# A chunked recurrence's scores: 128-key products against products of 32 keys, scores cleared once

## The chip, the cores and the metric

One core of one Trainium2 chip. The metric is the time of one execution on the device in microseconds (us), the median of the runs; lower is better.

## What is computed

One layer of a trunk on x (1, 2048, 1024), in f32: a normalised input projection into differential attention and a gated linear recurrence, an output projection, and a gated feed-forward layer. The recurrence is the part that the change touches:

```python
# per head, chunks of tokens; b = cumulative log of the forget gate, k = 1 - f
diff   = b[t] - b[s]
decay  = exp(where(t >= s, diff, -inf))
scores = einsum('tk,sk,tsk->ts', q, k, decay)
o      = einsum('ts,sv->tv', scores, v) + einsum('tk,kv->tv', q * exp(b), state)
state  = exp(b_last) * state + einsum('sk,sv->kv', k * exp(b_last - b), v)
```

There are 4 heads of 128 features. The kernel takes chunks of 128 tokens, 4 heads wide.

## The kernel before

The kernel has four stages in a row: `project` (input projection), `mix_tokens` (attention and recurrence, the stage of the change), `feed` (output projection and feed-forward) and `down`. Each stage has one program for each engine, written out by hand, and counted semaphores between them; an engine does its list in order. SyncE (SP) issues the DMAs.

**Attention in `mix_tokens`.** `for s in range(TOTAL + 2)` runs over 4 heads x 16 steps of 128 queries. In a step TensorE makes the scores of two maps (`score`, L1396 to L1399: f32r products with up to 512 keys into a ring of four PSUM banks; L1398 adds the chunk mask by a product of 64 loaded columns), VectorE takes maxima (L1259), ScalarE exponentials (L1148), VectorE combines the two maps (L1278), TensorE turns them (L1413), ScalarE copies them (L1157), and TensorE weighs the values (L1424).

**Recurrence in the same stage.** While attention works on head h (16 steps), the recurrence works on block h of 512 tokens (4 chunks of 128, all 4 heads). Its work is cut into 30 "fills", each of which TensorE writes into one PSUM bank and another engine reads. `FILLS` (L780) lists them: 4 diagonals, 7 levels x 2 sides (a side is 2 heads, so 8 head-chunks), 4 turned keys, and 4 pairs of output and state. Two fills go into each of the first 15 steps (`fill(h, 2 * j)` between the two maps' scores, `fill(h, 2 * j + 1)` after the first turns). For the first 8 fills of a block two banks are used in turn, `rec_fill` and the spare bank of the ring (in the trace `att_ring`); later ones have one bank.

The scores of a chunk are made by levels. At level m, j = 2^m: the queries in the right half of each run of 2j tokens meet the keys in the left half of the same run. GpSimd multiplies keys and queries in place by the forget factors between levels (L1127, L1129), and waits for the fill before (`fill_done`). TensorE (`fill`, L1441) makes for each of the 8 head-chunks one product: all 128 keys are loaded, and the 64 queries of the right halves are moved. Only at the last level (m = 6, L1464) are just 64 keys loaded. VectorE (`read_fill`, L1281) then writes the valid part into `rscore` by a predicated copy with a mask of the level (L1298); at the last level it is a plain copy (L1296). The diagonal fill (L1453) is 128 keys by 128 queries for each of a head's 4 chunks, and VectorE multiplies it by the identity (L1288), which writes the whole tile and so also clears it.

The lines that set the reading:

```python
tok = slice(c * C, (c + 1) * C)
queries = rq[:, head, tok].rearrange("p (n s j) -> p n s j", s=2, j=1 << at)[:, :, 1, :]
if at == LEVELS - 1:
    earlier = slice(c * C, c * C + RUN)
    last = pe.matmul(out[0:RUN, hc * RUN:(hc + 1) * RUN], rk[:, head, earlier], queries, start=True, stop=True)
    continue
dst = out[:, hc * RUN:(hc + 1) * RUN].rearrange("p (n j) -> p n j", j=1 << at)
last = pe.matmul(dst, rk[:, head, tok], queries, start=True, stop=True)
```

TensorE may write a fill when `fill_read` says that the one (or the one before) has been read. An f32 product appears in the trace as two pairs of a weight load (PEld) and a matmul (PE). In a product `matmul(out, lhsT, rhs)` lhsT is what is loaded, rhs what is moved. The trace writes "128\*64" for 128 rows and 64 loaded columns.

**Start of the stage.** VectorE clears `state` (L1340), makes `early_rows` and `late_keys` (L1341 to L1345, the small operands of L1398), then the two products for lambda (L1348). TensorE's first instruction waits for `masks_made` = 4, which the last of these memsets brings.

**Masks.** `make_level_masks` (L128), on GpSimd at the start of `project`, makes 7 masks of 128 x 512 bytes. GpSimd's next work in `project` waits for pieces of `w_out` (L492).

## Time and profile before

| what | value |
|---|---|
| median of 3 runs | 2718.12 us (2717.34 to 2718.37) |
| the profiled execution | 2718.51 us |
| its span | 2716.8 us |
| instructions | 34334 |
| mean granted TensorE clock | 0.987 |

All times below are from the one profiled execution. PE is TensorE's matmuls, PEld its weight loads (which overlap them), DVE is VectorE, ACT ScalarE, POOL GpSimd. A timeline row merges neighbouring instructions of one kind; its second number reaches from the first one's start to the last one's end, and x16 says how many. Matmuls are pipelined and their ends are modelled, so the distance between starts tells more than the duration of one. The clock is given as a share of full speed (2.4 GHz), and 0.50 is 1.2 GHz.

### The profile page before, as it was taken

Reading aid. Unit: us, or ns where it says so; the run is one execution under the profiler, and the core shown is the slowest. Engines: PE = TensorE matmul, PEld = TensorE weight load, DVE = VectorE, ACT = ScalarE, POOL = GpSimd, SP = SyncE. Lnnn points to the kernel's source line nnn. Section 1 sums busy time; section 2 is a strip of 40 time slices with the busy share of each in tenths; the row PEclk is TensorE's granted clock in tenths of the full one; section 3 lists DMA queues with packets and bytes.
Section 4 is the critical chain, followed back from the end, with each engine's and each line's share of the span. In section 5 each row is a group of like instructions: output and inputs, shape, how many; then the busy total and the mean of one; then the engine's idle time right before and its main releaser. Section 6 shows DMA issues by size and latency. Waiting matters only on the chain. (4 is left out here: it accounts for less than half of the span.)

```text
span 2716.8 us, 34334 instructions
## 1 busy us (share of the span) xinstructions
PE 2609.6 (96%) x13288; PEld 2202.3 (81%) x13288; DVE 1555.9 (57%) x1915; ACT 1141.3 (42%) x1917; POOL 906.2 (33%) x607
## 2 busy tenths in 40 slices
PE   7999999999899999997998999999999999999999
PEld 6888888887888888885877888887888887888887
DVE  5434344333676767675566666667666666356653
ACT  4434344332577676775554222224222223332221
POOL 5001100001515151403546445554554452236400
PEclk9999999999999999997999999999999999999999
DMA  4755556384443433306685333345343335777763
GB/s 159 263 184 194 177 201 202 124 273 126 121 111 94 123 96 101 109 21 216 228 278 169 95 103 108 101 116 183 101 116 96 103 109 158 262 271 275 238 204 130
DMA packets 343874, 430.48 MB, mean 158 GB/s; under 512 B 19232, under 2 KB 212768, under 8 KB 341024
## 3 DMA queue, kind: packets, MB, share of 16 engines
q1 hardware_dynamic: 343712, 428.29, 49.9%
q8 instruction: 106, 1.74, 0.3%
q14 instruction: 56, 0.46, 0.1%
HBM read 301.87 MB, written 129.50 MB: 159 GB/s over the span
## 5 line engine op out<-in xcount | busy, mean ns | idle before, releaser
L610 DVE TENSOR_TENSOR proj_w_lo<-proj_w_raw,proj_w_hi 128x2048 fp32r<-128x2048 f32 x56 | 130.3, 2326 | 230.0 <-ACT proj_w_hi L510 230.0
L757 PE MATMUL proj_prod<-proj_w_hi,proj_h_lo 128*128 128x512 f32 x640 | 250.1, 391 | 0.0
L1804 ACT ACTIVATE feed_a_hi<-lend_shared 128x1024 fp32r<-128x1024 f32 (+1 forms) x78 | 93.8, 1202 | 295.4 <-PE feed_v_bank L2103 142.0
L1148 ACT ACTIVATE att_expo<-att_ring,att_neg_max 128x1024 f32<-128x1024 f32 (+4 forms) x192 | 164.6, 861 | 92.4 <-DVE att_neg_max L1264 74.4
L2101 PE MATMUL feed_y_bank<-feed_b_hi,feed_a_hi 128*128 128x512 f32 x416 | 167.0, 401 | 15.3 <-DVE feed_results L1958 9.0
L2101 PE MATMUL feed_x_bank<-feed_b_hi,feed_a_hi 128*128 128x512 f32 x416 | 163.3, 392 | 12.7 <-DVE lend_lent L1927 11.0
L1804 ACT ACTIVATE feed_a_hi<-ahead_full 128x1024 fp32r<-128x1024 f32 (+1 forms) x78 | 93.4, 1202 | 186.4 <-PE feed_y_bank L2103 137.1
L2101 PE MATMUL feed_v_bank<-feed_b_hi,feed_a_hi 128*128 128x512 f32 x416 | 162.9, 392 | 5.0 <-DVE feed_results L1976 4.2
L2103 PE MATMUL feed_y_bank<-feed_b_hi,feed_a_lo 128*128 128x512 f32 x416 | 165.3, 397 | 0.0
L1922 DVE TENSOR_TENSOR feed_a_lo<-lend_shared,feed_a_hi 128x1024 fp32r<-128x1024 f32 (+1 forms) x78 | 147.3, 1888 | 31.4 <-ACT feed_a_hi L1804 31.4
L2103 PE MATMUL feed_x_bank<-feed_b_hi,feed_a_lo 128*128 128x512 f32 x416 | 162.8, 391 | 0.0
L2102 PE MATMUL feed_v_bank<-feed_b_lo,feed_a_hi 128*128 128x512 f32 x416 | 161.9, 389 | 0.0
L2103 PE MATMUL feed_v_bank<-feed_b_hi,feed_a_lo 128*128 128x512 f32 x416 | 161.9, 389 | 0.0
L1259 DVE TENSOR_REDUCE att_run_neg_max<-att_ring 128x1 f32<-128x1024 f32 (+7 forms) x128 | 121.2, 986 | 60.4 <-PE att_ring L1399 60.0
L510 ACT ACTIVATE proj_w_hi<-proj_w_raw 128x2048 fp32r<-128x2048 f32 x56 | 107.2, 1914 | 103.8 <-PE proj_prod L757 74.4
L1922 DVE TENSOR_TENSOR feed_a_lo<-ahead_full,feed_a_hi 128x1024 fp32r<-128x1024 f32 (+1 forms) x78 | 131.5, 1687 | 26.7 <-ACT feed_a_hi L1804 26.7
L757 PEld LDWEIGHTS proj_prod<-proj_w_hi,proj_h_lo 128*128 128x128 f32 x640 | 120.6, 188 | 25.7
L162 POOL TENSOR_TENSOR ahead_full<-ahead_full 128x512 f32<-128x512 f32 x26 | 33.7, 1296 | 306.0 <-DMA ahead_full<-in_w_up_dram 271.7
L755 PE MATMUL proj_prod<-proj_w_hi,lend_lent 128*128 128x512 f32 x320 | 127.6, 399 | 7.0 <-DVE proj_w_lo L610 6.2
L755 PE MATMUL proj_prod<-proj_w_hi,proj_h_hi 128*128 128x512 f32 x320 | 125.7, 393 | 0.0
L756 PE MATMUL proj_prod<-proj_w_lo,lend_lent 128*128 128x512 f32 x320 | 125.3, 392 | 0.0
L756 PE MATMUL proj_prod<-proj_w_lo,proj_h_hi 128*128 128x512 f32 x320 | 124.5, 389 | 0.0
(319 smaller groups left out, 7220.3 us busy)
## 6 DMA issues: line engine op xcount, KB each, us to landing
proj_w_raw<-in_w_in_dram SPq DMA_DIRECT2D x56, 1024.0 KB, 6.5
lend_shared<-in_w_gate_dram SPq DMA_DIRECT2D x88, 256.0 KB, 3.9
ahead_full<-in_w_up_dram SPq DMA_DIRECT2D x88, 256.0 KB, 4.0
ff<-ahead_results SPq DMA_DIRECT2D x88, 256.0 KB, 2.6
ff<-ahead_ff_sum SPq DMA_DIRECT2D x66, 256.0 KB, 3.2
operands<-ahead_results SPq DMA_DIRECT2D x48, 256.0 KB, 3.1
lend_lent<-ff SPq DMA_DIRECT2D x28, 384.0 KB, 3.3
down_f_raw<-ff SPq DMA_DIRECT2D x28, 384.0 KB, 3.2
```

The costliest lines, as they stand in the source:

```text
L510: nc.scalar.activation(w_hi[n % 2][:], w_raw[n % 2][:], ACT.Copy).then_inc(w_hi_made, 1)
L610: nc.vector.tensor_tensor(w_lo[n % 2][:], w_raw[n % 2][:], w_hi[n % 2][:].bitcast(F32), ALU.subtract).then_inc(w_lo_made, 1)
L755: pe.matmul(prod[t][:], hi[:, s, tile], wh[:, k, :], start=start, stop=False)
L756: pe.matmul(prod[t][:], hi[:, s, tile], wl[:, k, :], start=False, stop=False)
L757: last = pe.matmul(prod[t][:], lo[:, s, tile], wh[:, k, :], start=False, stop=stop)
L1148: nc.scalar.activation(expo[b][:, m, key:key + width], ring[:, bank * 512:bank * 512 + width], ACT.Exp, bias=neg_max[:, b, m:m + 1], accum ...
L1259: last = nc.vector.tensor_reduce(dst, ring[:, bank * 512:bank * 512 + width], AX.X, ALU.max, negate=True)
L1804: nc.scalar.activation(a_hi[:, first:end], full[g % 2][:, first:end], ACT.Copy).then_inc(a_hi_made, 1)
L1922: nc.vector.tensor_tensor(a_lo[:, first:end], full[g % 2][:, first:end], a_hi[:, first:end].bitcast(F32), ALU.subtract).then_inc(a_lo_made, 1)
L2101: pe.matmul(dst, a_hi[:, pos, s, :], hi, start=opens and s == 0, stop=False, skip_group_check=True)
L2102: pe.matmul(dst, a_hi[:, pos, s, :], lo, start=False, stop=False, skip_group_check=True)
L2103: last = pe.matmul(dst, a_lo[:, pos, s, :], hi, start=False, stop=s == HALF_SLABS - 1, skip_group_check=True)
```

## The change

Within 32 tokens (levels 0 to 4) and on the diagonal, each product is cut into blocks of 32 keys by the 16 (levels) or 32 (diagonal) queries of the same 32 tokens; each block has a position in the array of its own (`tile_position`), 0, 32, 64 or 96, the rows of PSUM that it writes. Level 5 becomes two products of 32 keys by 32 queries for each head-chunk, level 6 stays one of 64 by 64. VectorE copies levels 5 and 6 without a mask, and the diagonal by a predicated copy with a mask of its own. Since nothing writes the zeros any more, `rscore` and the two banks are cleared once at the start of the stage. GpSimd makes 5 level masks and one of the diagonal.

```diff
+GRID = 32
+LOW_LEVELS = GRID.bit_length() - 1
@@ make_level_masks
-    for m in range(masks.shape[1]):
+    for m in range(LOW_LEVELS):
...
+    pool.wait_ge(made, steps)
+    nc.gpsimd.memset(work[:], 0.0).then_inc(made, 1)
+    pool.wait_ge(made, steps + 1)
+    view = work[:].rearrange("p (c n) -> p c n", n=P)
+    nc.gpsimd.affine_select(out=view, in_=view, compare_op=ALU.not_equal, fill=1.0, base=0, pattern=[[0, width // P], [-1, P]],
+                            channel_multiplier=1).then_inc(made, 1)
+    pool.wait_ge(made, steps + 2)
+    nc.gpsimd.tensor_copy(masks[:, LOW_LEVELS, :], work[:]).then_inc(made, 1)
@@ project, gpsimd
-            pool.wait_ge(mask_step, 4 * masks.shape[1])
+            pool.wait_ge(mask_step, 4 * LOW_LEVELS + 3)
@@ mix_tokens, vector, read_fill
                 if kind == "diagonal":
-                    nc.vector.tensor_tensor(rscore[:, side * HALF + at], src.rearrange("p (c t) -> p c t", t=C),
-                                            ident[:].unsqueeze(1).to_broadcast([P, CH, C]), ALU.mult).then_inc(fill_read, 1)
+                    nc.vector.copy_predicated(rscore[:, side * HALF + at], mask[:, LOW_LEVELS].rearrange("p (c t) -> p c t", t=C),
+                                              src.rearrange("p (c t) -> p c t", t=C)).then_inc(fill_read, 1)
...
-                    if at == LEVELS - 1:
-
-                        nc.vector.tensor_copy(dst[0:RUN], src[0:RUN].rearrange("p (n j) -> p n j", j=RUN)).then_inc(fill_read, 1)
+                    if at >= LOW_LEVELS:
+
+                        j, whole_rows = 1 << at, rscore[:, side * HALF:(side + 1) * HALF].rearrange("p h c n -> p (h c) n")
+                        for n in range(C // (2 * j)):
+                            rows = slice(2 * j * n, 2 * j * n + j)
+                            last = nc.vector.tensor_copy(whole_rows[rows, :, 2 * j * n + j:2 * j * (n + 1)],
+                                                         src[rows].rearrange("p (c n j) -> p c n j", c=HC, j=j)[:, :, n, :])
+                        last.then_inc(fill_read, 1)
                         return
@@ mix_tokens, vector, start
             nc.vector.memset(state[:], 0.0)
+
+            nc.vector.memset(rscore[:], 0.0).then_inc(scores_cleared, 1)
+            for bank in fill_banks:
+                nc.vector.memset(bank, 0.0).then_inc(scores_cleared, 1)
+            dve.wait_ge(scores_cleared, 3)
             nc.vector.memset(early_rows[:].bitcast(F32), 0.0).then_inc(masks_made, 1)
@@ mix_tokens, tensor, fill
                 if kind == "diagonal":
                     head = side * HALF + at
-                    for c in range(CH):
-                        tok = slice(c * C, (c + 1) * C)
-                        last = pe.matmul(out[:, tok], rk[:, head, tok], rq[:, head, tok], start=True, stop=True)
+                    for at in range(0, TB, GRID):
+                        tok, rows = slice(at, at + GRID), slice(at % C, at % C + GRID)
+                        last = pe.matmul(out[rows, tok], rk[:, head, tok], rq[:, head, tok], start=True, stop=True, tile_position=(0, rows.start))
...
                     for hc in range(HC):
                         head, c = side * HALF + hc // CH, hc % CH
-                        tok = slice(c * C, (c + 1) * C)
-                        queries = rq[:, head, tok].rearrange("p (n s j) -> p n s j", s=2, j=1 << at)[:, :, 1, :]
-                        if at == LEVELS - 1:
-                            earlier = slice(c * C, c * C + RUN)
-                            last = pe.matmul(out[0:RUN, hc * RUN:(hc + 1) * RUN], rk[:, head, earlier], queries, start=True, stop=True)
+                        j = 1 << at
+                        if at >= LOW_LEVELS:
+                            for n in range(C // (2 * j)):
+                                first = 2 * j * n
+                                last = pe.matmul(out[first:first + j, hc * RUN + n * j:hc * RUN + (n + 1) * j], rk[:, head, c * C + first:c * C + first + j],
+                                                 rq[:, head, c * C + first + j:c * C + first + 2 * j], start=True, stop=True)
                             continue
-                        dst = out[:, hc * RUN:(hc + 1) * RUN].rearrange("p (n j) -> p n j", j=1 << at)
-                        last = pe.matmul(dst, rk[:, head, tok], queries, start=True, stop=True)
+                        for n in range(C // GRID):
+                            first = c * C + n * GRID
+                            queries = rq[:, head, first:first + GRID].rearrange("p (n s j) -> p n s j", s=2, j=j)[:, :, 1, :]
+                            dst = out[n * GRID:(n + 1) * GRID, hc * RUN + n * GRID // 2:hc * RUN + (n + 1) * GRID // 2]
+                            last = pe.matmul(dst.rearrange("p (n j) -> p n j", j=j), rk[:, head, first:first + GRID], queries,
+                                             start=True, stop=True, tile_position=(0, n * GRID))
@@ mix_tokens, tensor
                 if fills:
+                    if s == 0:
+                        pe.wait_ge(scores_cleared, 3)
@@ hybrid_trunk_kernel
-                masks = Alloc(nc, both, "level").sb("masks", [P, HGRN_LEVELS, HEADS // 2 * TB // 2], mybir.dt.uint8)
+                masks = Alloc(nc, both, "level").sb("masks", [P, LOW_LEVELS + 1, HEADS // 2 * TB // 2], mybir.dt.uint8)
```

## Rows read from the trace of the kernel before

**Rows 1.** The page, part 1: engine, busy time (share of the span) and instructions.

```profile
PE 2609.6 (96%) x13288; PEld 2202.3 (81%) x13288; DVE 1555.9 (57%) x1915; ACT 1141.3 (42%) x1917; POOL 906.2 (33%) x607
```

**Rows 2.** Windows: busy time of each engine in 50 us stretches.

```profile
core 0: us, PE busy (x) PEld busy (x) DVE busy (x) ACT busy (x) POOL busy (x), PEclk, DMA share, GB/s
...
700.00:750.00 50.00, 44.65 (x344) 40.12 (x343) 32.80 (x58) 28.93 (x73) 21.09 (x21) 1.00 0.17 50
...
1150.00:1200.00 50.00, 48.55 (x365) 44.98 (x365) 39.35 (x71) 36.28 (x83) 2.35 (x1) 1.00 0.06 22
```

**Rows 3.** Windows over the level fills of the second block.

```profile
807.00:835.00 28.00, 26.59 (x218) 24.82 (x216) 19.34 (x36) 22.82 (x66) 18.49 (x14) 1.00 0.61 166
835.00:864.00 29.00, 27.10 (x227) 25.09 (x227) 17.80 (x30) 19.64 (x49) 14.83 (x15) 1.00 0.39 110
```

**Rows 4.** Waits of PE, 700 to 1200 us: total us, times, longest.

```profile
PE att_ring L1396 <- ACT att_expo L1148: 24.2, 19, 1.8
PE att_turned L1413 <- DVE att_expo L1278: 3.5, 10, 0.7
```

**Rows 5.** Timeline, level fills 5 and 6: start us, us, engine line op.

```profile
852.34 1.86 PEld L1467 LDWEIGHTS rec_fill<-lend_shared 128*128 128x128 f32 x16
852.45 1.90 PE L1467 MATMUL rec_fill<-lend_shared 128*128 128x64 f32 x16
...
856.48 0.40 PE L1399 MATMUL att_ring<-att_k_rest,lend_lent 128*128 128x512 f32 x1
...
856.72 0.22 PE L1396 MATMUL att_ring<-att_k_rest,lend_lent 128*128 128x128 f32 x1
856.72 0.13 PEld L1398 LDWEIGHTS att_ring<-att_late_keys,att_early_rows 128*64 128x64 f32 x1
856.78 0.19 PE L1398 MATMUL att_ring<-att_late_keys,att_early_rows 128*64 128x64 f32 x1
856.78 0.19 PEld L1399 LDWEIGHTS att_ring<-att_k_rest,lend_lent 128*128 128x128 f32 x1
856.81 0.30 PE L1399 MATMUL att_ring<-att_k_rest,lend_lent 128*128 128x128 f32 x1
...
857.04 1.01 PEld L1464 LDWEIGHTS rec_fill<-lend_shared 128*64 128x64 f32 x16
857.04 1.15 PE L1464 MATMUL rec_fill<-lend_shared 128*64 128x64 f32 x16
```

**Rows 6.** Timeline of PE around a diagonal fill of the third block.

```profile
937.80 1.06 PE L1453 MATMUL rec_fill<-lend_shared 128*128 128x128 f32 x8
938.62 0.30 PE L1396 MATMUL att_ring<-early_k,lend_lent 128*128 128x128 f32 x1
```

**Rows 7.** Source lines L1453, L1467 and L1464: ns min/median/max, first and last start.

```profile
L1453 PE MATMUL rec_fill<-lend_shared x64: 272/275/423, 665.8 to 1083.9; 128*128 128x128 f32 x64
...
L1453 PE MATMUL att_ring<-lend_shared x64: 275/275/522, 667.6 to 1085.3; 128*128 128x128 f32 x64
...
L1467 PE MATMUL rec_fill<-lend_shared x640: 217/275/415, 676.1 to 1130.1; 128*128 128x64 f32 x160
...
L1467 PE MATMUL att_ring<-lend_shared x128: 222/273/274, 678.8 to 1097.7; 128*128 128x64 f32 x128
...
L1464 PE MATMUL rec_fill<-lend_shared x128: 222/222/270, 719.7 to 1139.1; 128*64 128x64 f32 x128
```

**Rows 8.** Timeline at the start of the stage.

```profile
664.51 0.48 DVE L1340 MEMSET rec_state<- 128x512 f32 x1 [20.02 <-PEq L295]
...
664.96 0.11 DVE L1341 MEMSET att_early_rows<- 128x64 f32 x1
...
665.29 0.11 DVE L1345 MEMSET att_late_keys<- 1x64 f32 x1
...
665.46 0.33 PE L1396 MATMUL att_ring<-early_k,lend_lent 128*128 128x128 f32 x1 [4.25 <-DVE att_late_keys L1345]
```

**Rows 9.** Windows around that start; PEclk is the granted clock.

```profile
661.00:665.50 4.50, 0.25 (x2) 0.04 (x1) 0.92 (x6) 1.76 (x2) 0.49 (x1) 1.00 0.17 62
666.30:669.70 3.40, 3.40 (x20) 3.40 (x18) 2.86 (x11) 0.97 (x5) 3.01 (x6) 0.50 1.21 321
669.70:673.10 3.40, 1.73 (x15) 1.53 (x14) 3.30 (x7) 0.71 (x4) 2.71 (x3) 1.00 1.00 199
```

**Rows 10.** Source lines L1288, L1298, L1296: DVE reads of fills; who waited.

```profile
L1288 DVE TENSOR_TENSOR rec_score<-rec_fill,all_ident x8: 681/686/692, 668.5 to 1084.2; 128x512 f32<-128x512 f32 x8
...
L1298 DVE COPY_PREDICATED rec_score<-level_masks,rec_fill x40: 699/722/1353, 678.2 to 1130.4; 128x512 f32<-128x512 uint8 x40
L1298 DVE COPY_PREDICATED rec_score<-level_masks,att_ring x8: 1303/1332/1355, 680.7 to 1098.0; 128x512 f32<-128x512 uint8 x8
...
  PE att_ring L1396: 0.8, 1
...
L1296 DVE COPY rec_score<-rec_fill x8: 677/680/683, 722.9 to 1139.3; 64x512 f32<-64x512 f32 x8
```

**Rows 11.** Timeline of POOL: end of the masks, and the next work.

```profile
38.62 0.61 POOL L148 CAST level_masks<-proj_mask_work 128x512 uint8<-128x512 f32 x1
129.96 1.30 POOL L493 TENSOR_TENSOR proj_mask_work<-early_rf 128x512 f32<-128x512 f32 x1 [90.74 <-DMA early_rf<-in_w_out_dram]
```

More of the change, by code:

```diff
@@ L962, in mix_tokens @@
         fill_read = r.sem("fill_read")
+        scores_cleared = r.sem("scores_cleared")
         q_ready = [r.sem(f"q_ready{h}") for h in range(2)]
```

## The prediction

> **What bounds the kernel now.** The page comes first: TensorE is busy for 96% of the span [rows 1], so the question is what the change does to TensorE's own time. The mixing stage, where all edits but the masks lie, runs from 665 to about 1230 us. The windows show TensorE busy for 44.65 of 50 us at its beginning and for 48.55 at its end, with VectorE at 33 to 39 and ScalarE at 29 to 36 of the 50 [rows 2]. Over the level fills of the second block TensorE is busy for 26.59 of 28 and 27.10 of 29 us, so it stands still for 3.3 us a block, 13 us in four [rows 3]. The waits say what ends its idle time: mostly the exponentials that must free a bank of the score ring, 24.2 us in 500 [rows 4]. TensorE's program order is therefore the path, with a cushion of some 3 us a block.
>
> **What a fill costs on TensorE.** I read this as cadence, not as busy time. A product in f32 is two pairs of weight load and matmul: the 48 level fills before the last level have 8 products each and show 640 + 128 = 768 matmuls, and the 16 diagonal fills of 4 products show 64 + 64 = 128 [rows 7]. In the timeline 16 weight loads of 128 columns take 1.86 us [rows 5]. One lasts 0.19, so their starts are (1.86 - 0.19) / 15 = 111 ns apart. The last level loads 64 columns and moves the same 64 queries: (1.01 - 0.14) / 15 = 58 ns [rows 5]. Both move 64 columns, so it is the loaded width that sets the pace: 53 ns for 64 columns more, or 0.83 ns a column, and 5 ns that are fixed. The diagonal moves 128 columns behind 128 loaded, and 8 pairs pass in 938.62 - 937.80 = 0.82 us, 103 ns each, again about the pace of the load [rows 6]; I count 111.
>
> **Low levels and diagonal, new cadence.** No row has 32 loaded columns. The line through the two widths gives 58 - 27 = 31.5 ns a pair. That is my value, since the nearer row (64 columns) and the line agree on the slope. The bounds: 58 / 4 = 15 ns, if the four key blocks of a product are loaded side by side, and 58 ns, the shortest pair of the trace, if a pair costs that much whatever its width.
> - Low levels: 5 levels, 2 sides, 4 blocks, 40 fills. Each had 16 pairs, 1.78 us; each gets 8 x 4 products, 64 pairs, 64 x 31.5 = 2.02 us. That is +0.24 each and +9.5 us.
> - Diagonals: 16 fills, 8 pairs at 111 (0.89 us) become 32 pairs, 1.01 us: +1.9 us.
> - Level 5: 8 fills. 16 pairs at 111 (1.78 us) become 16 products of 32 keys by 32 queries, 32 pairs, 1.01 us: -6.2 us. Its n = 0 and n = 1 products stand in rows 0 to 31 and 64 to 95.
> - Level 6 is the same product under another expression: nothing.
> The four pieces load as many columns as the one product did, so the narrower moving side saves nothing while the load sets the pace; only level 5, which now loads half the keys, gains. Net +5.2 us on TensorE.
>
> **Start of the stage.** VectorE's memsets release TensorE's first score: TensorE waits 4.25 us for the last of them (L1345) [rows 8]. The new memsets stand ahead of L1341. From the start of L1340 to that of L1341 512 elements take 0.45 us [rows 8]; the scores have 2048 a partition, 1.8 us, each bank 512, 0.45 to 0.5 (PSUM, where no memset is shown; the state's is the nearest). With the wait: 2.9 us, all on the path, between 2.5 and 4. Queued behind it on VectorE are the lambda products and the first maxima, and ScalarE waits for those, so all of them move together. The granted clock was 0.50 (1.2 GHz) from 666.3 to 669.7, after TensorE had only 0.25 us of work from 661 to 665.5, and TensorE was busy for the whole 3.40 us [rows 9]. The longer gap may bring more of such a stretch: between nothing and half of 3.4 us of work, 1.7. I take 0.9.
>
> **What is off the path.** The diagonal's read goes from 686 ns to a predicated copy like the levels', 722 ns at the median and 1353 at most [rows 10]: 16 x 0.04, at most 16 x 0.67 = 11 us of VectorE, which has over a quarter of the stage free; TensorE waited for such a read only once, 0.8 us [rows 10]. Level 5's read becomes two copies of 32 x 256. By the level copy's 680 ns for 512 elements [rows 10], less 256 at the state memset's 0.94 ns an element [rows 8], each costs 0.44, 0.88 against 0.72, eight times. With that cover gone they would cost 2 us, 12 at most. GpSimd's masks end at 39.2 us and its next work starts at 129.96 [rows 11]: two level masks fewer and one for the diagonal move nothing, with 90 us to spare. No DMA is added or moved.
>
> **The sum.** 5.2 + 2.9 + 0.9 = +9.0 us. The profiled execution took 2718.51 us (span 2716.8), so 2727.5; it lies 0.4 over the median of the runs, so against that I say 2727.1 us. About 0.2% (5.4 us) is what a measurement of this kernel tells from no change: "same" is 2712.7 to 2723.5.
>
> **A rule against the rows.** A 64-column matmul (L1398) already stands between full ones. It starts 60 ns after L1396 and the next L1399 starts 30 ns later, while L1396 still runs: changing the width costs nothing there [rows 5]. The Trainium skill, TensorEngine Tiling (Array Packing), Key Properties, says that changing the tiling mode drains TensorE; by it each fill would pay at both ends and the sum would be that of the third rival, 2750 us, where the row alone gives 2727. The row can't settle it, since L1398 gives no position in the array and the new products do.
>
> **Rivals.**
> 1. **The pieces run side by side (31%).** The four key blocks of a product use four column groups, in turn. If they overlap fully, a pair costs 15 ns: low fills 64 x 15 = 0.93 us, -0.85 x 40 = -34; diagonals 0.47, -0.42 x 16 = -7; level 5 has two groups, 29 ns, 0.93 us, -0.85 x 8 = -7. That is -48. ScalarE is busy for 22.8 of 28 us there [rows 3], so the waits for its exponentials would grow; three quarters, -36, and +3.8 for the start gives 2686 us. For it: the load's pace is the bound now, and only overlap lifts it. Against it: no row shows two loads under way at that pace. It decides below 28 ns a pair. By the same page of the Trainium skill, Key Properties, different tiles load and multiply in parallel; the trace neither agrees nor disagrees.
> 2. **The pair has a floor (14%), the other side.** If issuing the pair costs 58 ns whatever its width, low fills take 64 x 58 = 3.71 us (+1.93 x 40 = +77), diagonals 1.86 (+0.97 x 16 = +15), level 5 1.86 (+1): +93, less the cushion of 13, +3.8: 2802 us. It makes the kernel slower from 32 ns on. For it: 2432 pairs are added to 13288. Against it: 58 and 111 lie on a line in the loaded width with 5 ns left over, so a floor must lie just under 58 by chance.
> 3. **Each positioned fill drains TensorE (18%).** On entering, the tail of the last score, 0.40 - 0.24 = 0.16 us; on leaving, the tail of the last product, 0.22 - 0.03 = 0.19, and a load of 0.11 that can't go ahead. 0.46 x 64 fills = 29, some 6 of it in the cushion: +23 on top of my sum, 2750 us. The durations are those of [rows 5, 7]; against it is the row of L1398 above.
> 4. **Nothing that counts (4%).** The cushion takes the 5 us, and the memsets hide behind a load or a wait at the start: 2719 us. Against: the wait at the start names L1345.
>
> **Numbers.** My sum gets 33%: its own range, cadence 28 to 36 ns and start costs 2.5 to 6, is 2715 to 2738. In it I give 3 of the 33 to faster, 6 to same, 24 to slower. Faster 0.34, same 0.10, slower 0.56. The range takes in the sum, rivals 1, 3 and 4 and mixtures (overlap with drains, a floor near 40 ns): 2684 to 2775. Left out are rival 2's end and the far side of rival 1.
>
> **What would show each step.** Weight loads of 32 columns in the timeline: a low fill of 64 pairs should take about 2.0 us from the first load to the next line's; under 1.8 speaks for rival 1, 3.7 for rival 2. The next score's start against the last product's end, and no load ahead of it, shows rival 3. TensorE should start 2.9 us later after L1345. A second stretch at granted clock 0.50 after 669.7 would show the clock term. The forecast is wrong if the cadence at 32 columns is not on the line of the two widths.

## The result and the profile after

The changed kernel takes **2722.62 us** (median of 20 runs, 2717.20 to 2726.86) against 2717.09 us for the kernel before (20 runs, 2711.85 to 2723.61). The ratio is 1.0021, 95% interval 1.0014 to 1.0027: 5.5 us slower. The forecast was 2727.1 us, so the sign and roughly the size are right. The reason given for them is wrong, as the rows show.

TensorE's row on the page, after:

```profile
PE 2571.4 (95%) x15720; PEld 2149.0 (79%) x15720; DVE 1554.8 (57%) x1926; ACT 1141.8 (42%) x1917; POOL 901.8 (33%) x602
```

Against [rows 1] TensorE is busy for 38 us **less**, with 2432 matmuls more (29 us less in e1, a second profiled execution of the same kernel). The forecast had it busy for 5 us more. So the puzzle is the reverse of the one that I prepared for: where did a gain of this size go?

Windows of after: the first 40 us of the mixing stage, and the whole stage, from the end of the projection to the first product of the feed-forward.

```profile
core 0: us, PE busy (x) PEld busy (x) DVE busy (x) ACT busy (x) POOL busy (x), PEclk, DMA share, GB/s
665.00:705.00 40.00, 24.09 (x569) 19.50 (x569) 23.66 (x51) 11.94 (x35) 24.93 (x21) 0.59 0.96 238
661.80:1245.20 583.40, 486.69 (x6434) 428.60 (x6432) 396.86 (x723) 390.02 (x945) 192.66 (x156) 0.94 0.39 105
```

The same of before:

```profile
665.00:705.00 40.00, 36.27 (x271) 34.47 (x271) 29.06 (x59) 16.17 (x48) 29.20 (x25) 0.91 0.95 237
660.90:1240.30 579.40, 521.23 (x4002) 478.76 (x4000) 394.72 (x712) 389.89 (x945) 193.06 (x156) 0.98 0.38 105
```

Two things are to be seen. The stage has 34.5 us less of TensorE's work, and takes 4 us longer. And its first 40 us went badly: TensorE is busy for 24.1 of 40 us instead of 36.3, at a mean granted clock of 0.59 instead of 0.91.

**The fills.** Weight loads of the new products in the stage, by form, after:

```profile
L1493 PEld LDWEIGHTS rec_fill<-lend_shared 128*32 128x32 f32 x2048 | 22.9, 118 | 16.0 <-issue 11.9 <-DVE rec_score L1315 3.3
L1493 PEld LDWEIGHTS att_ring<-lend_shared 128*32 128x32 f32 x512 | 6.5, 132 | 4.2 <-issue 3.6 <-DVE rec_score L1315 0.7
L1486 PEld LDWEIGHTS rec_fill<-lend_shared 128*32 128x32 f32 x256 | 4.7, 112 | 1.6 <-issue 1.0 <-DVE rec_score L1311 0.7
L1475 PEld LDWEIGHTS att_ring<-lend_shared 128*32 128x32 f32 x256 | 3.2, 122 | 1.5 <-issue 1.4
L1475 PEld LDWEIGHTS rec_fill<-lend_shared 128*32 128x32 f32 x256 | 3.1, 122 | 1.1 <-DVE rec_score L1300 0.2
```

and those of the same fills before:

```profile
L1467 PEld LDWEIGHTS rec_fill<-lend_shared 128*128 128x128 f32 x640 | 75.8, 192 | 1.5 <-issue 0.6
L1467 PEld LDWEIGHTS att_ring<-lend_shared 128*128 128x128 f32 x128 | 14.9, 192 | 0.0
L1453 PEld LDWEIGHTS att_ring<-lend_shared 128*128 128x128 f32 x64 | 9.4, 227 | 0.0
L1453 PEld LDWEIGHTS rec_fill<-lend_shared 128*128 128x128 f32 x64 | 8.1, 199 | 0.0
```

108.2 us of loading became 40.4. Single fills, from the timeline of the weight loads, after:

```profile
844.69 0.64 PEld L1493 LDWEIGHTS rec_fill<-lend_shared 128*32 128x32 f32 x64 [0.17 <-DVE rec_score L1315]
...
861.40 0.59 PEld L1486 LDWEIGHTS rec_fill<-lend_shared 128*32 128x32 f32 x32 [0.17 <-DVE rec_score L1311]
```

One such load lasts 106 ns at least, so 64 pairs start (0.64 - 0.106) / 63 = **8.5 ns** apart, 32 pairs of level 5 (0.59 - 0.106) / 31 = 15.6 ns. The diagonal's 32 take 0.35 us in the third block, 7.9 ns a pair. At the half clock of the first block 64 pairs take 0.91 to 0.95 us, about 12 ns each. The sum had 31.5.

### The profile page after: what moved, and what is told of

Its sections match the earlier page's. It is cut to its first block and busy times, and to the rows that moved or that the text cites. A ratio compares the mean times of both kernels' runs of the same rounds, so it can differ in the third digit from the quotient of the medians.

```text
span 2715.5 us, 39206 instructions
## 1 busy us (share of the span) xinstructions
PE 2571.4 (95%) x15720; PEld 2149.0 (79%) x15720; DVE 1554.8 (57%) x1926; ACT 1141.8 (42%) x1917; POOL 901.8 (33%) x602
```

## The experiments

Each median stands beside runs of the kernel before on the same chip, and two kernels are compared by their ratios to it. Times of a stage, a step or a fill are from one profiled execution of each kernel. A "step" is the time from one reciprocal of VectorE to the next, one for each of the 16 steps of a block. Over the levels it holds the second fill of one level and the first fill of the next.

### As it is, and the start

**e1_after**: the changed kernel, no edit.

> The changed kernel as it is, on the chip of the three runs below, so that they can be held against it. Expected: 5 to 6 us slower than the kernel before, a low fill of 64 pairs in about 0.95 us, and waits of TensorE for nothing that the profile shows (issue) of over 15 us in the mixing stage.

2721.94 us, ratio 1.0020 (1.0011 to 1.0029). From the last projection matmul to the first of the feed-forward it took 586.0 us, before 579.5. The loss is in this stage. (The profile shown above is of the fastest of its 20 executions; its stage took 583.5.) The 0.95 us expected for a low fill is the price at half clock; at full clock it is 0.64.

**e2_clear_elsewhere**: the scores are cleared by GpSimd ahead of its first product, the banks and the state by VectorE behind the small operands that TensorE's first score waits for.

> The changed kernel, but the scores are cleared by GpSimd ahead of its first product, and the two banks and the state by VectorE behind the small operands that TensorE waits for. If the memsets stand on the path at the start of the stage, TensorE starts about 3.8 us earlier and the kernel is 2.5 to 4 us faster than the changed one (GpSimd had 2.6 us to spare before its first update in the kernel before). If the start is hidden later by the waits of the first steps, the time is that of the changed kernel within 1 us.

```diff
+            nc.gpsimd.memset(rscore[:], 0.0).then_inc(rscore_cleared, 1)
...
-            nc.vector.memset(rscore[:], 0.0).then_inc(scores_cleared, 1)
```

2720.79 us, ratio 1.0016 (1.0008 to 1.0025): 1.1 us better than e1 by the ratios, less than their intervals, and less than the 2.5 to 4 us expected. VectorE at the start says why. The changed kernel:

```profile
666.26 1.76 DVE L1359 MEMSET rec_score<- 128x2048 f32 x1 [0.38 <-issue]
...
669.57 0.11 DVE L1367 MEMSET att_late_keys<- 1x64 f32 x1
669.61 0.20 DVE L1370 CUSTOM_DVE_ANT_0 early_lams<-early_lams 128x64 f32<-128x64 f32 x1
...
670.66 0.29 DVE L1271 TENSOR_REDUCE att_neg_max<-att_ring 128x1 f32<-128x128 f32 x1
```

e2:

```profile
665.90 0.11 DVE L1363 MEMSET att_late_keys<- 1x64 f32 x1
...
667.74 1.89 DVE L1369 CUSTOM_DVE_ANT_0 early_lams<-early_lams 128x64 f32<-128x64 f32 x1
...
670.91 0.29 DVE L1273 TENSOR_REDUCE att_neg_max<-att_ring 128x1 f32<-128x128 f32 x1
```

The first score starts 4 us earlier, but the first maximum, which releases ScalarE, no earlier: a lambda product that takes 0.20 us in the changed kernel takes 1.89 us beside a product on GpSimd. The kernel before paid that too (1.66 us at 665.33). So counted at the first maximum the memsets cost 1.5 us (8.95 us behind the projection's last matmul, 7.45 before), though TensorE starts 3.4 us later.

### What sets the pace of a pair

**e3_one_position**: every piece of the low levels goes to column group 0, with the same number and size of products. Only the overlap of the groups is gone, and with it the scores of three pieces in four, which are left out.

> The changed kernel, but all four blocks of a low-level product go to position 0 and rows 0 to 31 of the bank, so three of four blocks overwrite the wrong place; the same number of pairs, of the same sizes. If the pairs pass in 15 ns because four column groups load and multiply side by side, one position alone brings the pace of my line, about 31 ns a pair, 2.0 us a low fill instead of 0.95: TensorE gets 40 us more work, and the kernel is 5 to 25 us slower than the changed one. If a narrow pair is cheap by itself, the pace stays at 13 to 15 ns and so does the time.

```diff
-dst = out[n * GRID:(n + 1) * GRID, hc * RUN + n * GRID // 2:hc * RUN + (n + 1) * GRID // 2]
+dst = out[0:GRID, hc * RUN + n * GRID // 2:hc * RUN + (n + 1) * GRID // 2]
...
-                 start=True, stop=True, tile_position=(0, n * GRID))
+                 start=True, stop=True, tile_position=(0, 0))
```

2762.78 us, ratio 1.0155 (1.013 to 1.018). A fill of 64 pairs:

```profile
838.80 2.10 PEld L1493 LDWEIGHTS rec_fill<-lend_shared 128*32 128x32 f32 x64
```

(2.10 - 0.11) / 63 = 31.6 ns a pair: the line through the two widths was right to 0.1 ns, for one group. With four groups it is 8.5, little more than a quarter of it. The positions are what makes the pieces cheap.

**e4_load_32**: the kernel before, but its levels 0 to 4 load 32 keys of 128, without positions. The scores of the other 96 keys are left out. Same count of instructions as before, and no clearing.

> The kernel before, but at levels 0 to 4 only the first 32 of the 128 keys of a chunk are loaded (no position is given); the scores of the other keys are left out. As many instructions as before, no clearing. It frees TensorE of about as much time as the change does, (1.78 - 0.5) x 40 = 50 us. Theory A (the freed time is mostly off the path, because the steps then wait for VectorE's and ScalarE's results): 8 to 20 us faster than before. Theory B (the freed time is on the path, and the change loses it only to the late start and to missing instructions): 35 to 50 us faster. The pace of an unplaced pair with 32 loaded columns is also seen here: my line says 31.5 ns, or 53 / 2 = 27 ns more if the 64 moved queries set it, that is 58.

```diff
-dst = out[:, hc * RUN:(hc + 1) * RUN].rearrange("p (n j) -> p n j", j=1 << at)
-last = pe.matmul(dst, rk[:, head, tok], queries, start=True, stop=True)
+keys = 32 if at < 5 else C
+dst = out[0:keys, hc * RUN:(hc + 1) * RUN].rearrange("p (n j) -> p n j", j=1 << at)
+last = pe.matmul(dst, rk[:, head, c * C:c * C + keys], queries, start=True, stop=True)
```

```profile
835.85 0.92 PEld L1468 LDWEIGHTS rec_fill<-lend_shared 128*32 128x32 f32 x16 [0.18 <-issue]
```

(0.92 - 0.11) / 15 = 54 ns. 32 keys loaded and 64 queries moved take about what 64 and 64 took (58, [rows 5]), and not the 31.6 of 32 and 16, so by these widths a pair takes what the **larger** of its two sides takes. The kernel takes 2708.5 us, ratio 0.9969 (0.9957 to 0.998), 8 us less. In the stage TensorE is busy for 22 us less (499.1 against 521.1), and the stage is 7.9 us shorter (571.7 against 579.5). About two thirds of what these fills free isn't on the path, without a single instruction added. The waits show where it goes: that for VectorE's rows grew by 10.1 us, that for ScalarE's copy by 2.6.

**e5_grid_64**: blocks of 64 keys, two column groups: 32 pairs a fill instead of 64. Level 5 is then one of the placed levels too, with 64 loaded keys instead of 32. **e6_grid_64_clear** adds to it the clearing of e2, with the memsets of the banks behind the lambda products.

> The changed kernel with blocks of 64 keys by 32 queries (64 on the diagonal) at two positions instead of four blocks of 32: half the pairs, 32 a low fill. By the pace seen (58 ns a pair of 64 columns alone, two column groups side by side) a low fill takes 32 x 29 = 0.93 us, the same as with four blocks. Theory 1 (what the change loses in the first block is TensorE waiting for its instructions, and the low clock): the waits for nothing that the profile shows fall from 27 us to under 15, and the kernel is 4 to 8 us faster than the changed one, near the kernel before. Theory 2 (the loss is the late start and the waits for other engines alone): same as the changed kernel within 2 us.

> As the run with blocks of 64, and the clearing is taken off the start: GpSimd clears the scores ahead of its first product, VectorE clears the banks and the state behind its lambda products, which then don't run beside a GpSimd product (0.2 us each where they took 1.7 to 1.9). The first maximum should come 7 us or less after the last product of the projection (9.0 in the changed kernel, 7.45 before): 2 us faster than the run with blocks of 64. If the start is hidden by later waits, the same within 0.7 us.

```diff
-GRID = 32
+GRID = 64
```

```profile
835.72 1.01 PEld L1493 LDWEIGHTS rec_fill<-lend_shared 128*64 128x64 f32 x32
```

(1.01 - 0.14) / 31 = 28 ns a pair, half of 58: two groups overlap as four do. e5 takes 2719.84 us, 1.0013 (1.0004 to 1.0021), 1.9 us better than e1 by the ratios. Its waits for nothing that the profile shows did shrink, from 17.9 us in e1 to 3.1, but the 4 to 8 us that were expected with them didn't come; its fills are longer (1.01 us against 0.64, and 1.01 against 0.59 at level 5). e6 takes 2715.87 us, 0.9999 (0.9991 to 1.0008). In e6 the lambda products are through before GpSimd's product starts, the first maximum comes 6.3 us behind the projection instead of 8.95, and the kernel is 3.8 us faster than e5 by the ratios. It is level with the kernel before.

### Where the freed time goes

The waits of TensorE over the stage, before:

```profile
PE att_ring L1396 <- ACT att_expo L1148: 25.7, 20, 1.8
PE att_turned L1413 <- DVE att_expo L1278: 6.8, 13, 1.7
PE att_out L1424 <- ACT att_wt L1157: 4.3, 9, 1.8
PE att_ring L1396 <- DVE att_late_keys L1345: 4.3, 1, 4.3
...
PE att_out L1424 <- issue: 2.0, 3, 0.7
```

and after:

```profile
PE att_ring L1418 <- ACT att_expo L1160: 25.6, 20, 1.8
PE att_turned L1435 <- DVE att_expo L1290: 21.3, 26, 1.8
PE att_out L1446 <- ACT att_wt L1169: 9.6, 18, 1.8
PE rec_fill L1493 <- issue: 8.3, 4, 3.1
PE att_ring L1418 <- DVE att_late_keys L1367: 7.6, 1, 7.6
PE att_out L1446 <- issue: 7.1, 3, 4.1
PE att_ring L1493 <- issue: 2.3, 2, 1.3
```

The waits for the score ring are unchanged. What grew is the wait for VectorE's combined softmax rows (+14.5) and for ScalarE's copy (+5.3): TensorE finishes its fill, and the turned block that comes next isn't ready, because the chain score, maximum, exponential, sum, combination of the step is no shorter. That takes 20 us of the gain. "Issue", where TensorE waits for nothing that the profile shows, went from 2.0 to 17.7, and the start took 3.3. Together 38.8 us: the 34.5 that TensorE is less busy, and the 4 that the stage is longer.

How little a step gains is plain where the second fill of level 4 and the first of level 5 lie: both are shorter by about 0.95 us from score to score, and the step goes from 8.83 to 8.28 us. Where the long fill did end last, in the step with the second fill of level 5 and the first of level 6, more comes through. The reciprocals around that step in the second block, before:

```profile
849.96 0.17 DVE L1272 RECIPROCAL att_inv<-att_total 128x2 f32<-128x2 f32 x1
...
858.62 0.17 DVE L1272 RECIPROCAL att_inv<-att_total 128x2 f32<-128x2 f32 x1
```

and after:

```profile
858.83 0.17 DVE L1284 RECIPROCAL att_inv<-att_total 128x2 f32<-128x2 f32 x1
...
866.54 0.17 DVE L1284 RECIPROCAL att_inv<-att_total 128x2 f32<-128x2 f32 x1
```

8.66 us became 7.71, with one fill shortened in it.

### The first block

Here the step with the second fill of level 2 and the first of level 3 went from 6.73 to 15.48 us (13.11 in e1). The weight loads of that stretch, after:

```profile
696.41 0.84 PEld L1493 LDWEIGHTS rec_fill<-lend_shared 128*32 128x32 f32 x54 [3.19 <-issue]
...
704.87 1.78 PEld L1446 LDWEIGHTS att_out<-lend_lent,att_wt 128*128 128x128 f32 x8 [4.18 <-issue]
```

TensorE stands for 3.2 and 4.2 us, and no engine or DMA that the profile shows ends the wait. At that time the DMA queues of after look so (685 to 706 us; the first row is the busy share in 40 slices, in tenths, the others a queue's packets, MB and share of the 16 engines):

```profile
DMA  9999999999999999999999999999999951100000
...
q1 hardware_dynamic: 3967, 4.67, 88.6%
q8 instruction: 3, 0.05, 1.0%
```

The profile names one of these queues "instruction", and I take it that the program comes through it. It moved 3 packets of 16 KB where before it moved 1, and 125 instead of 106 in the whole span. They share the engines with 4.7 MB of data, partly loads for the next block. Before the engines were about as full in this stretch (83.5% of the time for queue q1), without such waits.

**e7_late_loads** moves the loads for the next block only: SP issues the features, the first keys and the values of block 1 behind step 8 of block 0. Nothing else changes.

> The changed kernel, with three loads of 1 MB each for the next block (keys, values, forget factors) issued after the eighth step of the first block instead of at its start. Theory 1a (TensorE's instructions come late because their packets stand behind the data of the full queues, DMA share 1.0 from 665 to 700 us): TensorE's waits for nothing that the profile shows shrink in the first block from about 16 us to under 6, and the kernel is 4 to 8 us faster than the changed one. Theory 1b (they come late at any load, since 128 instructions a fill are used up in 1 us): the waits stay, same time within 2 us.

```diff
+                if h == 0:
+                    sp.wait_ge(q_ready[1], 2)
+                    load_features(sp, mid["hf"], 1, rf[:], rf_in)
+                    load_first_k(1)
+                    load_v(1)
```

2713.31 us, ratio 0.9994 (0.9985 to 1.0003); 7.1 us better than e1 by the ratios. Over the same 21 us, e7:

```profile
DMA  9996110100194697979763000000100000000010
...
q1 hardware_dynamic: 975, 1.83, 31.1%
q8 instruction: 4, 0.07, 1.4%
```

With the queues free the same step takes 7.13 us, though the queue "instruction" moves no less (4 packets). In the stage "issue" falls from 17.9 us in e1 to 11.3. That the waits called "issue" are waits for the program is argued from this, not shown. Shown is that those of this stretch need the full DMA queues; what the other 11 us need, no run shows.

**e8_all**: e6 and e7 together.

> Blocks of 64, the clearing off the start and the late loads together. If all three losses are what they seem, what is left is the gain of the kernel that loads 32 of 128 keys (8 us faster than before) and the earlier first maximum: 8 to 12 us faster than the kernel before. If the losses overlap, 3 to 8 us.

2715.58 us, ratio 1.0000 (0.9991 to 1.0008). Expected were 3 to 12 us faster than before; it should have beaten both and didn't. With 32 pairs a fill there is little waiting for the program to remove (3.1 us in e5). Its interval overlaps that of e7, and I can't say more.

**The granted clock** of the first 40 us (665 to 705), from the windows of each kernel:

| kernel | TensorE busy, of 40 us | granted clock |
|---|---|---|
| before | 36.27 | 0.91 |
| after | 24.09 | 0.59 |
| e3, all at one position | 35.55 | 0.57 |
| e5, blocks of 64 | 34.72 | 0.62 |
| e6, blocks of 64, cleared elsewhere | 38.75 | 0.55 |
| e7, late loads | 29.32 | 0.66 |
| e4, 32 keys loaded, unplaced | 33.56 | 0.96 |
| e9, first block as before | 36.33 | 0.96 |
| e11, level 5 only | 35.88 | 0.91 |

The others fit in: 0.60 in e1, 0.59 in e2, 0.67 in e8, 0.96 in e10 and 0.91 in e12. The low stretch goes with the pieces in the first block and not with TensorE's idle time: e6 is busier than any other and has the lowest clock.

```profile
670.00:690.00 20.00, 20.00 (x196) 16.52 (x195) 13.20 (x25) 6.46 (x21) 16.33 (x16) 0.50 1.04 251
```

That is e6, busy without a gap for 20 us at half clock. In the changed kernel the granted clock was 0.50 (1.2 GHz) from 664.8 to 685.3, where before it came back at 669.7 [rows 9].

**e9_first_block_whole**: block 0 works as before (whole products, no clearing), blocks 1 to 3 as changed. **e10_first_whole_64**: the same with blocks of 64.

> The changed kernel, but in the first of the four blocks of tokens the diagonal and levels 0 to 4 are made as before: whole products of 128 keys, the diagonal multiplied by the identity. That writes all of the scores and both banks, so no clearing is needed at all. Theory: the change loses in the first block (late first maximum, 1.5 us; TensorE waits for its instructions while the DMA queues are full; granted clock 0.5 for 20 us and more) and gains about 1.5 to 2 us in each later block. Then the first block is as before with less at level 5, the clock there is 0.50 for 3.4 to 7 us only, and the kernel is 3 to 6 us faster than the kernel before. If the low clock comes from something else than the placed pieces, it stays for 20 us and more, and the kernel is no faster than before.

> As the run above, and in the later blocks pieces of 64 keys by 32 queries at levels 0 to 4 (64 by 64 on the diagonal), level 5 in halves of 32 as in the change. Half the instructions for the same time on TensorE, so fewer waits for instructions: 5 to 8 us faster than the kernel before. If the later blocks' time is set by VectorE and ScalarE alone, the same as the run above within 1.5 us.

```diff
+                    if h == 0:
+                        for c in range(CH):
+                            tok = slice(c * C, (c + 1) * C)
+                            last = pe.matmul(out[:, tok], rk[:, head, tok], rq[:, head, tok], start=True, stop=True)
+                    for at in range(0, TB if h else 0, GRID):
```

e9 2713.67 us, 0.9990 (0.9981 to 0.9999); e10 2712.55 us, 0.9987 (0.9978 to 0.9996). Both beat the kernel before, by less than the 3 to 6 and 5 to 8 us expected. Against e1 the first block was worth 0.0030 of 2717, 8 us: all of the loss and more.

### Only the part that pays

**e11_level_5_only**: the kernel before, with level 5 alone as two products of 32 keys by 32 queries. It has no masks, positions or clearing; each product is read by a plain copy.

> The kernel before, with one part of the change: level 5 as two products of 32 keys by 32 queries for each head-chunk, copied without a mask. My sum gave -6.2 us for it at 31.5 ns a pair; the step that holds it was 0.96 us shorter in every block of the changed kernel, so 3 to 5 us faster than before, with no more stretches at low clock than before. If the step is not shorter here, that saving came from the low levels.

```diff
-                    if at == LEVELS - 1:
+                    if at >= LEVELS - 2:
```

2711.24 us, ratio **0.9979** (0.997 to 0.9989), with e12 the best of those that compute all scores. The level-5 step, between reciprocals at 849.11 and 856.81, takes 7.70 us as in the changed kernel, and it does so in each of the four blocks: 4 x 0.96 = 3.8 us. The step before it, which holds the other fill of level 5, stays at 8.83. TensorE is busy for 2598.5 us, only 11 less than before: 11 us freed give 5.7 by the ratio, where the whole change frees 38 and loses 5.5. The 1.9 us between 3.8 and 5.7 lie within the interval.

**e12_level_5_start**: e11 with GpSimd's first product held until two lambda products are through, and the state cleared behind them.

> The kernel before with level 5 in halves (the run above), and the start of the stage mended: GpSimd's first product waits for VectorE's two lambda products, and VectorE clears the state behind them instead of ahead of the small operands. In the kernel before the first lambda product takes 1.66 us beside a GpSimd product; alone it takes 0.2. So the first score comes 0.45 us earlier and the first maximum about 5.5 us after the projection's last product instead of 7.44. If that distance is on the path, 1.5 to 2 us faster than the run above, about 7 us faster than the kernel before; if GpSimd's later first product is on the path instead (it had 2.6 us to spare), no faster than the run above.

2710.77 us, 0.9979 (0.9971 to 0.9988). The first maximum came 0.9 us earlier than before (2 were expected); against e11 the kernel gained nothing that its interval shows. Inconclusive.

### The balance

By the ratios, each kernel against before on its own chip:

| part | from | us |
|---|---|---|
| level 5 in halves, all blocks | e11 | -5.7 |
| low levels and diagonals in blocks 1 to 3 | e9 less e11 | +3.0 |
| first block: placed pieces and the clearing | e1 less e9 | +8.2 |
| sum | | +5.5 |

The middle line is smaller than its two intervals together, so only indicated; in the profiled executions blocks 2 to 4 take 405.4 us in e9 and 401.5 in e11. A trace gives one reason for it: e4, whose low levels are short in all blocks, needs 9.46 us for a step in its second block and 7.91 for the same step in its third. The two steps as windows, e4:

```profile
812.32:821.78 9.46, 8.03 (x71) 6.93 (x68) 6.67 (x8) 5.99 (x18) 7.52 (x6) 0.82 0.65 178
949.48:957.39 7.91, 6.48 (x71) 5.47 (x68) 6.70 (x9) 5.87 (x18) 7.36 (x6) 1.00 0.53 168
```

Before it was 8.07 (reciprocals at 817.25 and 825.32). The short fills save 0.16 us there and lose 1.4 when the clock falls. Such dips stand at the beginning of later blocks in the changed kernel too (0.94 in 800 to 830, 945 to 975 and 1080 to 1110 us); e11 has none from 800 to 1200 us (granted clock 1.00 throughout). Another may be "issue", 10.3 us in e9 against 2.0 in e11.

## Why the prediction was right or wrong

**"TensorE's program order is the path."** Too strong. It holds where a fill of 1.9 us stands last in a step. When the fill gets shorter the step's softmax chain ends it, 0.55 us earlier where two fills had shed 0.95 each. [Rows 3] showed a cushion of 3.3 us a block, but that is idle time, which says how much longer TensorE may get; how much shorter it may usefully get is the slack of the other engines, and that I didn't read. I took TensorE's busy share for it.

**Cadence, the failed step.** "58 - 27 = 31.5 ns a pair" is the price of one column group (31.6 in e3), and the change uses four: 8.5 ns. The bounds of 15 to 58 didn't even contain it, since the lower one divided the pair of 64 keys by four, and not that of 32. The loads of a low fill went from 1.86 us to 0.64 at full clock, but what TensorE saves is read from the starts of the scores around it. The first fill of level 4 in the second block, before:

```profile
839.49 0.41 PE L1399 MATMUL att_ring<-att_k_rest,att_q_lh 128*128 128x384 f32 x1
839.75 1.89 PE L1467 MATMUL rec_fill<-lend_shared 128*128 128x64 f32 x16
841.45 0.47 PE L1396 MATMUL att_ring<-att_k_first,att_q_hl 128*128 128x512 f32 x1
```

From score to score that is 1.96 us, and after it is 1.01 (848.91 to 849.92, shown at rival 3). Low fills: forecast +9.5 us, measured 40 x -0.95 = -38. Level 5: -6.2, measured 8 x -0.97 = -8. Diagonals: +1.9, measured from 0.82 to 0.39 us, -7. Together -53 at full clock, where the forecast had +5.2. The stage shows 34.5 us less of busy time, because the attention's products (L1418 to L1460) are busy for 16 us more than before by the sums of their groups, about half of it in the first block with its half clock.

**"The loaded width sets the pace"** was read from rows that all had 64 columns moved. e4 shows the larger side to set it. Here that changes nothing, since the pieces move 16 or 32.

**Start: +2.9 on the path.** TensorE's first score came 3.4 us later, the size is right. But what the step waits for is the first maximum on VectorE, 1.5 us later, because the lambda product no longer ran into GpSimd's product.

**Clock: +0.9, at most 1.7.** The place was named, the size was not: 20.5 us at 0.50 in one piece, and a mean of 0.62 between 660 and 710, which is 38 us at 0.50, where the 0.93 of before is 7. I had tied it to the gap ahead of the first score; e6 shows it with a gap no longer than before's (3.71 us against 4.25) and with TensorE busy.

**Instruction supply** wasn't in the sum: 2432 more matmuls were counted only as time on TensorE. "Issue" waits of 17.7 us in the stage stand against them. What they cost isn't settled: e7 sheds 6.6 us of them and the kernel gains 7, e5 sheds 14.8 and it gains 1.9, with longer fills.

**VectorE's reads** were right: the diagonal's copy takes 732 ns (forecast 722), the copies of level 5 402 to 422 (forecast 440), and no matmul waits long for them (0.8 us in the stage). The masks moved nothing.

**Rival 1** (31%) has the right mechanism. By it the kernel should take 2686 us. The pairs do overlap: 31.6 ns at one position, 8.5 at four. The rule of the Trainium skill (TensorEngine Tiling (Array Packing), Key Properties) is that different tiles load and multiply in parallel; the trace agrees. "Three quarters realised" is where it failed. e4 realises a third, the changed kernel nothing.

**Rival 2** (a floor of 58 ns) is refuted by 8.5 ns.

**Rival 3** (a drain at each placed fill, 2750 us) had a price of 0.46 us a fill. The timeline of TensorE around one, after, shows less than half of it:

```profile
848.91 0.42 PE L1421 MATMUL att_ring<-att_k_rest,att_q_lh 128*128 128x384 f32 x1
849.26 0.74 PE L1493 MATMUL rec_fill<-lend_shared 128*32 128x16 f32 x64
849.92 0.50 PE L1418 MATMUL att_ring<-att_k_first,att_q_hl 128*128 128x512 f32 x1
```

The fill starts 0.35 us behind the last score's start, where before it was 0.26. The next score starts 0.66 us behind the fill's start, and 63 pairs of 8.5 ns are 0.54 of that: 0.12 behind the last pair, before 1.70 - 15 x 0.111 = 0.03. So a placed fill does pay, but some 0.2 us, and both 0.95 and 1.01 above hold it. e4's fills, which give no position, show the same (0.35 in front, 0.20 behind). The Trainium skill (TensorEngine Tiling (Array Packing), Key Properties) says that a change of tiling mode drains TensorE. The trace shows no drain of the size that rival 3 gave it; whether the 0.2 us are one isn't shown, since no run tells the mode apart from the loaded width.

**What the number rests on.** +9.0 was forecast from +5.2 (cadence), +2.9 (start), +0.9 (clock). The +5.5 measured are -5.7 from level 5 (there the forecast is right, by another way) and +11.2 from the first block and the low levels, where the forecast had +15.2 for them, but from a slower cadence that doesn't exist and not from the clock and the waits. A number near the mark is no support for the working.

**Open.** How the 8 us of the first block divide between the half clock and the waits for the program: e7 recovers 7, but its clock was also a little higher (0.66 against 0.60 in e1). What the 11 us of "issue" that e7 keeps are, and why e5, which has nearly none, gains so little. What in the pieces keeps the clock down: e3 excludes the overlap of four groups at the levels, e5 the number of 64 pairs and the moved side of 16 columns. Giving a position at all, a moved side of 32 or less and 32 or more pairs remain; e4, with neither positions nor more pairs, is at 0.96 there and has only the short dips. Late loads weren't tried on the kernel before, nor with e11; in the kernel before the step that e7 mends had no such wait to remove.

## What to carry to other kernels

Before shortening the busiest engine's work, read what the other engines of the same step would allow: the highest busy share says who is the bound, not how far below it the next one lies. Take the part of a change whose work ends a step last and measure it alone; here one of the six changed levels brought all the gain that is shown, and the rest gave it back. Splitting products into many small ones was cheap in time on TensorE and dear in what came with it: waits for nothing that the profile shows where the DMA queues were full, and a granted clock of 0.50.

## What the runs showed that I had not expected

- Products placed in different column groups overlap almost fully, loads and all: 31.6 ns a pair in one group, 8.5 with 32 keys in four; 58 with 64 keys in one, 28 in two.
- A pair of load and matmul took what the larger of loaded and moved columns takes: 54 ns for 32 loaded and 64 moved, 58 for 64 and 64, 31.6 for 32 and 16.
- A fill that loads 32 columns between products that load 128 costs some 0.2 us beyond its pairs, whether a position is given or not.
- With small placed products the granted clock stayed at 0.50 for 20 us, in e6 although TensorE was busy without a gap (20.00 of 20 us).
- With the DMA engines full, TensorE stood up to 4.2 us for nothing that the profile shows; with the loads put off the same stretch (685 to 706 us) had no such wait above 1.6 us.
- A VectorE product of 64 columns takes 0.20 us alone and 1.66 to 1.89 us beside a product on GpSimd.
